# A rebuilt beginning and a rebuilt router in a two-layer diffusion step: first norm placed among the modulation halves, router steps merged, first expert weights loaded earlier

## The reference, cut to what matters

```python
# 128 context tokens and 256 latent tokens, width 1024, two layers
for l in range(2):
    mod = silu(cond) @ w_ada[l] + b_ada[l]          # cond: c_ctx or c; 1024 x 6144
    sh1, sc1, g1, sh2, sc2, g2 = split(mod, 6)
    h = rmsnorm(x, norm1) * (1 + sc1) + sh1
    u = h @ w_in[l]                                  # conv | Fourier | RWKV-7 | gates
    x = x + g1 * (merged_branches(u) @ w_o[l])
    h = rmsnorm(x, norm2) * (1 + sc2) + sh2
    x = x + g2 * (dense_swiglu(h) if l == 0 else moe_swiglu(h))
def moe_swiglu(h):
    logits = h @ w_router + b_router                 # 8 experts
    top_v, top_i = top_k(logits, 2); p = softmax(top_v)
    return sum_e comb[:, e] * swiglu(h, w_gate[e], w_up[e], w_down[e])
y = rmsnorm(x, final_norm)
```

## Time and profile before

| | |
|---|---|
| median of 3 runs | 1922.8 us (1922.48 to 1926.27) |
| profiled execution | 1924.78 us |
| its span in the trace | 1923.0 us |
| PE busy | 1768.2 us (92%) |
| DVE, ACT, POOL busy | 1133.0, 906.2, 551.9 us |

### The profile page before, as it was taken

One profiled execution on the slowest core, in us unless ns is written; L12 is line 12 of the kernel. 1 busy time (PEld: TensorE's weight loads), 2 busy tenths in 40 slices (PEclk: granted clock), 3 DMA queues, 4 the chain that ended last, 5 costly groups with the idle time before them and its releaser, 6 DMA issues.

```text
span 1923.0 us, 40900 instructions
## 1 busy us (share of the span) xinstructions
PE 1768.2 (92%) x16511; PEld 1620.0 (84%) x16511; DVE 1133.0 (59%) x1645; ACT 906.2 (47%) x1362; POOL 551.9 (29%) x417
## 2 busy tenths in 40 slices
PE   4997979899999999999988889999699999999996
PEld 3996868799999999989978788999588788888885
DVE  0465687755331121034666885632498898989888
ACT  2445232243443333333532414344367777777775
POOL 0571000165556666656500004565100000000000
PEclk8898999999999999989989999999799999999998
DMA  9447133233424444433562001342588999999880
GB/s 303 117 131 229 60 92 96 82 110 121 142 82 129 132 132 132 130 95 106 172 202 84 5 4 58 110 132 88 203 284 296 312 307 316 313 322 307 299 295 33
DMA packets 225173, 315.31 MB, mean 164 GB/s; under 512 B 15614, under 2 KB 169604, under 8 KB 224900
## 3 DMA queue, kind: packets, MB, share of 16 engines
q1 hardware_dynamic: 217856, 306.22, 49.1%
q10 hardware_dynamic: 7172, 6.97, 1.3%
HBM read 311.05 MB, written 2.10 MB: 163 GB/s over the span
## 4 chain that ended last, share of the span: by engine, by line
PE 77%; DVE 12%; issue 4%; ACT 3%; DMA 2%; ACTq 1%; DVEq 0%; SPq 0%; POOL 0%
PE bank L598 75%; PE bank L595 3%; DVE e_w_rest L186 2%; DMA ring<-in_w_ada 2%; DVE S L1918 2%; DVE cvT L1821 1%; ACT e_w_rounded L1609 1%; DVE hT L1700 1%; DVE hT L1694 1%; DVE hg_rest L1730 1%; DVE U L1948 1%; DVE St L1970 0%; DMA xin<-in_x_sample 0%; DVE St L1967 0%; DVE tmp L1836 0%
## 5 line engine op out<-in xcount | busy, mean ns | idle before, releaser
L2299 POOL TENSOR_TENSOR weights_rest<-ring,weights_rounded 128x512 fp32r<-128x512 f32 x344 | 467.7, 1362 | 450.5 <-ACT weights_rounded L1297 449.6
L186 DVE TENSOR_TENSOR e_w_rest<-e_raw,e_w_rounded 128x1024 fp32r<-128x1024 f32 (+1 forms) x327 | 354.9, 1132 | 34.0 <-ACT e_w_rounded L1609 33.0
L1297 ACT ACTIVATE weights_rounded<-ring 128x512 fp32r<-128x512 f32 x344 | 215.5, 629 | 330.5 <-PE bank L598 322.3
L1609 ACT ACTIVATE e_w_rounded<-e_raw 128x1024 fp32r<-128x1024 f32 (+1 forms) x327 | 314.7, 989 | 78.8 <-PE bank L598 77.2
L598 PE MATMUL bank<-h_rounded,weights_rounded 128*128 128x384 f32 x688 | 231.3, 336 | 5.5 <-POOL h_rest L2313 2.8
L598 PE MATMUL bank<-h_rounded,weights_rest 128*128 128x384 f32 x688 | 229.9, 334 | 0.0
L598 PE MATMUL bank<-h_rest,weights_rounded 128*128 128x384 f32 x688 | 229.9, 334 | 0.0
L598 PE MATMUL bank<-e_w_rounded,hG_rounded 128*128 128x512 f32 (+1 forms) x432 | 164.4, 381 | 6.2 <-DVE e_w_rest L186 6.2
L598 PE MATMUL bank<-e_w_rest,hG_rounded 128*128 128x512 f32 (+1 forms) x432 | 162.2, 376 | 0.0
L598 PE MATMUL bank<-e_w_rounded,hG_rest 128*128 128x512 f32 (+1 forms) x432 | 161.6, 374 | 0.0
L598 PEld LDWEIGHTS bank<-h_rounded,weights_rounded 128*128 128x128 f32 x688 | 129.1, 188 | 8.8 <-DVE h_rest L1730 4.1
(11 more groups left out here) (346 smaller groups left out, 3615.3 us busy)
## 6 DMA issues: line engine op xcount, KB each, us to landing
ring<-in_w_ada SPq DMA_DIRECT2D x96, 512.0 KB, 5.8
e_raw<-in_moe_w_down SPq DMA_DIRECT2D x90, 512.0 KB, 4.7
ring<-in_w_in SPq DMA_DIRECT2D x88, 512.0 KB, 4.8
e_raw<-in_moe_w_gate SPq DMA_DIRECT2D x72, 512.0 KB, 5.5
e_raw<-in_moe_w_up SPq DMA_DIRECT2D x72, 512.0 KB, 6.9
e_raw<-in_moe_w_gate SPq DMA_DIRECT2D x36, 384.0 KB, 3.9
e_raw<-in_moe_w_up SPq DMA_DIRECT2D x36, 384.0 KB, 4.0
ring<-in_ffn_w_gate SPq DMA_DIRECT2D x22, 512.0 KB, 4.9
```

Source lines behind the costliest of these rows:

```text
L186: eng.tensor_tensor(wl, e_raw[n % E_RAW][:, 0:kn * w], wr.bitcast(F32), ALU.subtract).then_inc(s("e_rest"), 1)
L1297: a(w_parts[n % NSLOT][0], raw, ACT.Copy).then_inc(*E.up("rounded_ready", *key))
L1609: a(e_w[n % E_PARTS][0][:, 0:kn * w], e_raw[n % E_RAW][:, 0:kn * w], ACT.Copy).then_inc(s("e_rounded"), 1)
L2299: pool.tensor_tensor(wl, raw, wr.bitcast(F32), ALU.subtract).then_inc(*E.up("rest_ready", *key))
```

## The change

**Beginning.** `c` and `c_ctx` get a tile of their own (`crow`) and are ACT's first loads; then `first` and x. They are turned alone, so `condp` no longer waits for the vectors. The vectors of layer 0 are issued after the sigmoid, those of layer 1 after the squares, `second`, `wrt`, `brt` and the states after the first modulation. On PE the turning of x, the norm's sum, its row, and the turning of the vectors stand between the eight halves, with fillers. DVE scales all four groups of x before the modulation is there; afterwards only modulation and rests are left, all rests by DVE. SP loads the low-rank weights (`low`) before `z` block 4 instead of 0.

**Norms.** POOL adds more squares (sums of four or six tiles), for the second norm during the `w_o` product; PE sums three or four tiles instead of five.

**Router.** `wrt` and `brt` are loaded in layer 0. The logits come out with tokens as rows (24 calls, 8 columns each), in pairs of tiles as these are modulated; `lgT` and its turn go. The one-hot rows, weights and slot shifts are made by wider instructions, `rank` by 6 calls in place of 9, the weights after the slots. The `xtok` turning is spread; DVE does two of the six copies.

**Expert weights.** SP issues 14 of the first 18 pieces after the last rest of `merged`, the other 4 after `h2_ready`. ACT rounds pieces 0 and 1 around the root, 2 after the logits; POOL subtracts piece 0. `fin_row` is issued later. The warming matmuls ahead of the gather go.

```diff
             pe.wait_ge(*at("first_in"))
...
-                    pe.wait_ge(*at("cond_ready"))
-                    for i in range(4):
-                        for _ in ada(0, i):
-                            pass
+                    pe.wait_ge(*at("crow_in"))
+                    b = begin("cvec")
+                    transpose(b[:, 0:16], crow[0:16, :], 16).then_inc(*E.fill("cvec"))
+                    pe.wait_ge(*drained("cvec"))
+                    between = {0: lambda: filler(psum[7], 8), 1: lambda: filler(psum[7], 8), 2: x_transposes,
+                               3: lambda: norm_total(0, 0), 4: lambda: norm_row(0, 0, lambda: None),
+                               5: lambda: vectors(0), 6: lambda: vectors(1)}
+                    for n, _ in enumerate(half for i in range(4) for half in ada(0, i)):
+                        if n in between:
+                            between[n]()
+                        if n > 1:
+                            filler(psum[7], 4)
                     ada_turn(0, (0,))
+                    filler(psum[7], 16)
...
-                if key[0] == "z" and key[2:] == (0, 0):
+                if key[0] == "z" and key[2:] == (4, 0):
...
-            sp.wait_ge(*at("h2_ready", 1))
-            sp.wait_ge(*filled("o", 1, 7))
-            sp.wait_ge(*at("out_stored", "state", 1, 1))
+            sp.wait_ge(*at("x_parts", "merged", DEPTH - 1, 3))
...
+                    if job is None and n == BELOW_NORM:
+                        sp.wait_ge(*at("h2_ready", DEPTH - 1))
...
-            for k in range(KD):
-                last = mm(b[0:NE, 0:T], wrt[:, k, :], hT[:, k, :], k == 0, k == KD - 1)
+            for g in range(4):
+                pe.wait_ge(*at("h_odd", DEPTH - 1, 1, g))
+                pe.wait_ge(*h2_pair(g))
+                for k in (2 * g, 2 * g + 1):
+                    for j in range(3):
+                        last = mm(logit[:, j * NE:(j + 1) * NE], hT[:, k, j * P:(j + 1) * P], wrt[:, k, :],
+                                  k + j == 0, k == KD - 1 and j == 2)
...
+            def norm_total(l, which, meanwhile=None):
...
+                summands = (0, 6, 7) if which else (0, 4, 6, 7)
...
+                    root(l, 0)
+                    vectors(0)
+                    vectors(1)
                     ada_copies(0, (0,))
...
+                    convert(0)
+                    act.wait_ge(*at("modA_ready", l, 0))
+                    modulate(l, 0, between=convert)
+                    act.dma_start(second, dram["tables"][:, n_first:ncols]).then_inc(*E.up("second_in", by=16))
...
                 if l % 2 == 0:
                     start_phase(("fg", l), ("fu", l), ("fd", l))
+                if l == DEPTH - 1:
+                    e_round(0, 0, 1)
                 root(l, 1)
+                if l == DEPTH - 1:
+                    a(stat[:, 95:96], eps[1e-6], ACT.Sigmoid)
+                    e_round(0, 1, 2)
...
+                if meanwhile:
                     for g in range(4):
+                        scaled_x(l, which, g)
+                    meanwhile()
...
-            for j in range(3):
-                for t in range(3):
-                    ts(rt[:, R_SL + 24 * j + 8 * t:R_SL + 24 * j + 8 * t + 8], rk[:, 8 * j:8 * j + 8],
-                              -1.0 - P * t, None, A).then_inc(*E.step())
+            for t in range(3):
+                ts(by_slot(R_SL)[:, :, t, :], group(R_RK, 3), -1.0 - P * t, None, A).then_inc(*E.step())
...
+            select_weights(lambda at_: slice(at_, at_ + 1))
             hG_rest(0)
-            e_rests(0, 0, E_AHEAD)
+            dve.wait_ge(s("e_rest"), 1)
+            e_rests(0, 1, E_AHEAD)
...
-                rests(("o", l))
-                add_squares(l, 1)
+                rests(("o", l), count=10)
+                add_square(l, 1, 0, 1)
+                rests(("o", l), first=10, count=13)
+                add_square(l, 1, 2, 3)
+                rests(("o", l), first=13)
+                add_square(l, 1, 0, 2)
+                add_square(l, 1, 4, 5)
+                add_square(l, 1, 0, 4)
...
+            e_rest(pool, lambda name: sem(name).h, e_raw, e_w, 0, 0)
```

442 lines of the change are left out of this document (234 added, 208 removed).

## The result

The changed kernel takes **1913.7 us** (median of 12 runs, 1903.25 to 1922.93) where the kernel before, on the same chip, takes 1926.3 (median of 12, 1920.79 to 1931.5). The ratio is 0.9935, 95% interval 0.9915 to 0.9955: 12.6 us less, or between 9 and 16. The forecast was 1894 us with a range from 1886 to 1904. The kernel before came out 3.5 us above the median of the three runs that the forecast started from; the other 16 us are the forecast's. That it would be faster, held at 0.96, was right.

A forecast was written before the change was run, and what follows sets the result against it. PE was taken as the bound (busy 92% of the span), with time won where it waits or runs at half clock: front 11.5 + second norms 0.3 + router 16.9 = 28.7 us, giving 1894 us, range 1886 to 1904.

The forecast's parts named there:

- The front until the last half, and to the last group: Beginning: last modulation half ends at 42.0, last group of first `z` tile at 55.35 (before 67.48); front gains 11.5 us.
- Its remaining 18 matmuls: Layer 0's first norm sum: 18 PE matmuls behind POOL's additions, 0.21 or 0.11 us each, ending between 30.3 and 32.1.
- The rival of a slow front: PE at half clock to the end of the halves, at 51; front gives 2 us, total 1903.5; chance 0.10.
- After the groups ACT issues `second`, `wrt`, `brt` and the states, about 2.9 us ... so it stalls 0.7: First `z` tile: ACT's 2.9 us of issues precede its fourth piece, whose rest is ready at 59.2; PE stalls 0.7 us.
- a rival on small loads waiting for room: ACT's 30 small transfers each wait for queue room; at 2 us apiece 44 us lost, 1938; chance of slower 0.03.
- The loop itself is unchanged ... so the gain is kept: Expert loop: 527 us as before, not held by transfers at 281 GB/s, router gain kept; first pieces may shift 1 us.
- The router's sum: Layer 1's router up to the first expert matmul: 1379.1 for 1395.98, 16.9 us won, bounded by 14.2 and 18.7.
- The middle at -0.3: Second norm in layer 0: sum shrinks from 30 matmuls to 18, 0.3 us won; other middle stages keep their instructions.

## Why the prediction was wrong, by its steps

- **The front until the last half, and to the last group: right in the overlap, with luck in the size.** Its ends were forecast at 42.0 and 55.35 and came at 44.4 and 56.5; 11.0 us were won there. 44.4 is outside the step's own 39.8 to 43.4. "Its remaining 18 matmuls" had six too few behind POOL, so the sum ended 1.6 us behind the slow bound; the way from the last half to the last group was 1.2 us shorter than forecast, 0.9 of it because `modA` took 2.6 us for 3.55. The rival of a slow front did not come (1.08 us a half).
- **"After the groups ACT issues `second`, `wrt`, `brt` and the states, about 2.9 us ... so it stalls 0.7": wrong, and the largest miss.** The issues took 7.3 us and PE lost 4.1 us and some 1.5 more at half clock. The step priced each load by its own row in other surroundings. The runs with `wrt` moved, doubled neighbours and a compact copy show that its 1024 pieces of 32 bytes, issued behind `second` with the DMA engines full, hold the queue for the one behind. I had a rival on small loads waiting for room, and dismissed it by the vectors' rows; it comes nearest to what the one load that is not like them did.
- **"The loop itself is unchanged ... so the gain is kept": wrong by 3.5 us.** The instructions are; their operands' addresses are not. 2.7 us for eight jobs are shown to come from where `e_w` lies. The rest is small: with `e_w` back at its offset the whole loop takes 526.3 to 528.5 us in eight profiles, before 527.0.
- **The router's sum: right in mechanism, 2.95 us too good.** The logits ended 1.1 us late and the part behind them took 16.94 for 15.1. The step had the rank at half clock already (0.22 us a matmul), so that is not the miss. It left out the 1.32 us in which DVE loads the number of jobs, and the 1.0 us by which the job list is longer where POOL's zeroing still runs, as it does when the half level goes on through the turning (11 of 15 profiles); small steps that came 0.5 us sooner took some of it back. The two profiles that met the forecast's 30.3 us did so by luck: full clock on the rank and the small steps made up for the forgotten 1.3 us.
- **The middle at -0.3, since "the stages in the middle keep their instructions": their time did not stay.** It came at +4.1. It varies by 13 us between profiles of kernels with the same middle, and the forecast should have carried that spread in its range; but layer 1's scan is longer in every profile with the new beginning, and that cause is open.
- The absolute time also missed by 3.5 us in the base.

## What to carry to other kernels

Before moving a load to a busy stretch, look at its access pattern: count its pieces, not its bytes, and ask what is unfinished ahead of it on the queue, and what stands behind it there and on the engine that issues it. When buffers move, the code that uses them is not unchanged; compare the duration of one matmul in the hot loop before and after. And when single runs of one kernel differ by 20 us, cut the profiles at the same instructions and compare stretches, since the end-to-end median hides terms of 3 us in both directions.

## What was not expected of the hardware

- Behind a transfer of 1024 pieces of 32 bytes the next one took 4.98, 4.34 and 5.07 us on the queue (`brt`), or the next two 5.31 and 7.00 together (the states). As the last one it took 1.69 to 5.61 us itself, and 0.47 us at 140 us. In all the dear cases 1.7 MB on the same queue was unfinished and the DMA engines were 0.9 and more busy; at 140 us they were full too, but nothing else was on the queue, and at 1361 us, behind 0.5 MB and with the engines half busy, the next one took 0.50 us. The same 32 KB in 128 pieces took 0.45 us and cost its follower nothing.
- A float32 moving operand of 512 columns that starts 32 bytes past a multiple of 64 is read a little faster than one that starts at a multiple: 388 ns against 394 in the median of a group with some of 384 columns among them, 0.3 us in a job of 56. Seven profiles have the multiple and 56.1 to 56.2 us a job, ten (two of before among them) the offset and 55.8. Why is open.
- A stretch of router work with identical instructions takes 15.0 us behind the logits or 16.94, by TensorE's granted clock, though DVE's chain ends last in both. Half of the difference is PE's rank, which DVE waits for. The other half is on DVE: two instructions of 8 columns take 0.23 us alone and 1.20 us when POOL's memset of 128x3072 is running, ending with it, in all eleven such profiles.
